# RWKV inverse on folded 64x64 blocks in two array quarters, with sample products and chunk products in another order

## The chip, the cores and the metric

One core of a Trainium2 chip runs the kernel. The metric is the device time of the execution in microseconds: the median of 3 runs is 2621.8 us (2618.93 to 2631.11).

## What is computed

One layer of a streaming encoder on 256 prompt tokens and 8 sequences of 16 sample tokens (384 columns in all), D_MODEL 2048: RMSNorm, one combined input projection, an RWKV-7 branch (16 heads of 64), a latent-attention branch, gates, output projection, and a ConvGLU of width 5632. The change touches the RWKV branch alone. Its recurrence, for every head with a 64x64 state S:

```python
def step(S, inp):
    r_t, w_t, k_t, v_t, kk_t, a_t = inp
    sa = jnp.einsum('bhvk,bhk->bhv', S, kk_t)
    S = (S * w_t[:, :, None, :] + v_t[..., None] * k_t[:, :, None, :]
         - sa[..., None] * (kk_t * a_t)[:, :, None, :])
    return S, jnp.einsum('bhvk,bhk->bhv', S, r_t)
```

## The kernel before

The kernel does not step through tokens. It takes the prompt in 4 chunks of 64 tokens and the 8 sample sequences as chunks of 16. Within a chunk the effect of the a-term is a unit triangular matrix of token by token, whose inverse is needed. It is built by doubling: a block-diagonal inverse of blocks of 2, then 4, 8, 16, 32, 64, in five levels.

**The slice loop.** 16 heads are taken two at a time, one head in each half of the 128 partitions. `pe_rwkv` (L374), `act_rwkv` (L573) and `dve_rwkv` (L693) are the body of a slice on PE, ScalarE (ACT) and VectorE (DVE). It runs 8 times: 7 in a hardware loop, once more behind it with other projections beside it. All in it is fp32, except the projections.

**The pieces.** Beside a slice PE computes the projection columns of later slices, so that it has work while the others answer. `pieces(n)` (L1168) issues n of a slice's 32 pieces; each is 2 k-tiles of `pe_block` (L828), with three passes of 384 columns each (w_hi with x_hi L836, w_hi with x_lo L837, w_lo with x_hi L838). Four pieces use up half a weight tile. Its split is done on ACT (`act_hi` L816, L821) and DVE (`dve_lo` L823, L826), at `cut(k)`: eight per slice and engine, in the order written out by hand. The split of a half waits for the half two before it to be used; SP loads the raw half when the split on DVE is done with the last one. ACT also takes finished projections out of PSUM at even cuts. Where a `pieces(n)` stands in `pe_rwkv` decides what PE does while a wait runs; their order is fixed by hand. Before, they stand as 2, 1, 1, then one in each of five levels, 2, one in each of four chunks, 1, 2, 2, 4 and 8.

**The inverse.** A unit is one head i (0, 1) and one token tile t of 128 (t 0 and 1 hold two prompt chunks each, t 2 the samples): 6 units, 128x128, block-diagonal with two 64x64 blocks. L394 makes the strictly lower products of beta and alpha (64 rows, 128 columns out and in), L401 those of kappa and alpha. DVE masks the first into t_y (L709, L710) and n_t (L707). t_y is the inverse so far, t_x its transpose; both are kept up. PE transposes t_y (L315) and ACT copies it into t_x (L582). A level then is: G = n_t' t_x (L418), one piece, DVE masks G into t_g (L718), the update of t_x (L429, subtracted at L723) and that of t_y (L433, subtracted at L726), directly behind which stands the next level's G. Levels 0 to 2 take all 6 units, 3 and 4 only the prompt's 4; the last level updates t_y alone. Every product is 128x128 on the whole array. Then L438 makes c_k and c_b, masked by DVE.

**The chunks.** For each chunk c: r (L456, L459), a piece, u from the inverse (L471), and for both heads the state gain (`gain`, L483 and L490, 64 rows and 64 partitions out) and the output (`yo`, L484, L486, L488, L493, 128 rows and 64 partitions out). Chunk 0 has the samples' parts too: L464, L465, L477, L498, L499 and eight 16-column products a head (L501). L508 makes the samples' state gains in chunks 1 and 2. DVE turns r (L738), u (L750) and the state (L755 to L764) around between them.

**The samples' first products.** L388 multiplies 8 states with 16 columns each, for head 0 and then head 1, each into its own half of the output partitions.

Of the kernel before, what the change touches and what calls it, by code (L numbers as in the profile page):

```python
# [21 lines left out]
P = 128  # L22
# [25 lines left out]
C2 = ["bones", "st64", "st64", "st16", "in64", "in64", "in16", "nl1", "lv2", "lv4", "lv8", "lv16", "lv32"]  # L48
C3 = ["rot"]
NC1 = len(C1) * P  # L50
NC2 = len(C2) * P + NT + 8
# [13 lines left out]
def constants():  # L65
# [30 lines left out]
    out = cat(C1) + cat(C2) + [reset, bm] + cat(C3) + [np.cos(ang), np.sin(ang), amask]  # L96
# [25 lines left out]
def build(nc, a, consts, outs):  # L122
# [28 lines left out]
    with ctx:  # L151
# [26 lines left out]
        cm = {n: c2[:, i * P:(i + 1) * P] for i, n in enumerate(C2)}  # L178
        reset = c2[:, len(C2) * P:len(C2) * P + NT]
        bmask = c2[:, len(C2) * P + NT:NC2]  # L180
# [20 lines left out]
        n_t, t_x, t_y, t_g, m_t, c_k, c_b = [  # L201
            region(n, [P, 6, P]) for n in ("n_t", "t_x", "t_y", "t_g", "m_t", "c_k", "c_b")]
# [10 lines left out]
        half = lambda t, h: t[:, 3 * h:3 * h + 3, :].rearrange("p u c -> p (u c)")  # L213
        yb, yc, sq_y, rn_y = half(t_g, 0), half(t_g, 1), half(t_x, 0), half(t_x, 1)
# [86 lines left out]
        BON = cm["bones"]  # L301
# [40 lines left out]
        units = lambda lv: [(i, t) for t in range(3 if lv < 3 else 2) for i in range(2)]  # L342
# [8 lines left out]
        each = lambda m, n: m.unsqueeze(1).unsqueeze(1).to_broadcast([P, 2, n, P])  # L351
        both = lambda m: m.unsqueeze(1).to_broadcast([P, 2, 3, P])
# [21 lines left out]

        def pe_rwkv(f, pieces, more=True):
# [30 lines left out]
            for i, t in units(0):  # L406
                last = transpose(head_tile(2, i, t), t_y[:, 3 * i + t, :])
            last.then_inc(E("t_x_ps"), 1)
            pieces(1)
            pe.wait_ge(E("nt_done"), f + 1)  # L410
            for lv in range(5):
                if lv == 0:
                    pe.wait_ge(E("t_x_done"), f + 1)
                else:
                    pe.wait_ge(E("t_done"), f * 9 + (2 * lv - 1))
                for i, t in units(lv):
                    u = 3 * i + t
                    last = mm_(head_tile(g_bank(lv), i, t), n_t[:, u, :], t_x[:, u, :], start=True, stop=True)  # L418
                last.then_inc(E("g_ps"), 1)
                pieces(1)  # L420
                pe.wait_ge(E("g_done"), f * 5 + (lv + 1))
                if lv == 0:
                    pe.wait_ge(E("mt_done"), f + 1)
                else:
# [6 lines left out]
                for i, t in units(lv):  # L431
                    u = 3 * i + t
                    last = mm_(head_tile(2, i, t), t_g[:, u, :], t_y[:, u, :], start=True, stop=True)  # L433
                last.then_inc(E("dt_ps"), 1)

            for b, src in ((4, kp_), (6, be)):
                for i, t in units(0):
# [3 lines left out]
            pe.wait_ge(E("t_done"), f * 9 + 9)  # L441
# [7 lines left out]
            for c in range(4):  # L449
# [20 lines left out]
                for i in range(2):  # L470
                    last = mm_(ps[r0:r0 + 64, 3, heads(i)], t_y[:, 3 * i + t, cs], rr[:, 0, heads(i)],  # L471
                               start=True, stop=True)
                last.then_inc(E("u_ps"), 1)
                if c == 0:
                    pe.wait_ge(E("rd_done"), f + 1)
                    for i in range(2):
                        last = mm_(ps[:, 7, heads(i)], t_y[:, 3 * i + 2, :], rr[:, 1, heads(i)], start=True, stop=True)  # L477
# [15 lines left out]
                mm_(yo[1], un[:, 0, heads(1)], c_b[:, 3 + t, cs], start=False, stop=True).then_inc(E("y_ps"), 1)  # L493
                if c == 0:
                    pe.wait_ge(E("ud_done"), f + 1)
                    for i in range(2):
# [3 lines left out]
                        for b in range(NB):  # L500
# [32 lines left out]
            pieces(8)  # L533
# [39 lines left out]
        def act_rwkv(f, cut, ch, more=True):  # L573
# [7 lines left out]
            act.wait_ge(E("t_x_ps"), f + 1)  # L581
            fn(t_x[:, :, :].rearrange("p (h t) c -> p h (t c)", h=2), ps[:, 2:4, 0:NT], ACT.Copy).then_inc(E("t_x_done"), 1)  # L582
# [4 lines left out]
            cut(2)  # L587
# [7 lines left out]
            cut(3)  # L595
# [1461 lines left out]
```

## Time and profile before

| what | value |
|---|---|
| median of 3 runs | 2621.8 us |
| profiled execution | 2617.77 us |
| its span, first to last instruction | 2616.1 us |
| PE busy | 2551.1 us, 98% |
| DVE busy | 1201.2 us, 46% |
| ACT busy | 848.4 us, 32% |
| GpSimd (POOL) busy | 108.4 us, 4% |
| mean granted TensorE clock | 0.995 |
| products of the inverse's levels L418, L433, L429 (records) | 416, 416, 352 |

In a window's row stand its start and end, its length, the busy time of PE, PEld, DVE, ACT and POOL with their instructions in brackets, the granted clock, the DMA share and GB/s.

Times in the rows are microseconds from the start of the span. PE is TensorE's matmul, PEld its weight load, which runs beside it. In the timeline a row is one instruction or a run of like ones: start, length from the first start to the last end, engine, line, what is written and read, the shape (array rows x columns used, then the moving operand), and the count. Matmuls overlap: the pitch from start to start is what one costs in a stream, and the length has its latency too.

### The profile page before, as it was taken

Reading aid. Unit: us, or ns where it says so; the run is one execution under the profiler, and the core shown is the slowest. Engines: PE = TensorE matmul, PEld = TensorE weight load, DVE = VectorE, ACT = ScalarE, POOL = GpSimd, SP = SyncE. Lnnn points to the kernel's source line nnn. Section 1 sums busy time; section 2 is a strip of 40 time slices with the busy share of each in tenths; the row PEclk is TensorE's granted clock in tenths of the full one; section 3 lists DMA queues with packets and bytes.
Section 4 is the critical chain, followed back from the end, with each engine's and each line's share of the span. In section 5 each row is a group of like instructions: output and inputs, shape, how many; then the busy total and the mean of one; then the engine's idle time right before and its main releaser. Section 6 shows DMA issues by size and latency. Waiting matters only on the chain.

```text
span 2616.1 us, 40662 instructions
## 1 busy us (share of the span) xinstructions
PE 2551.1 (98%) x15484; PEld 2353.6 (90%) x15484; DVE 1201.2 (46%) x1855; ACT 848.4 (32%) x1247; POOL 108.4 (4%) x182
## 2 busy tenths in 40 slices
PE   6999999999999999999999899999999999999997
PEld 6888888888888999999987799999878999999886
DVE  4566566665644333334433444444333444444233
ACT  4332233322223333334422433333222333333232
POOL 3000000000001010000000000000000000000010
PEclk9999999999999999999999999999999999999999
DMA  5321222212244343334453344444333444444443
GB/s 171 90 63 43 55 68 69 67 40 60 61 104 123 104 121 101 102 90 129 127 168 121 96 128 127 123 127 128 121 121 130 127 125 124 128 128 126 143 126 129
DMA packets 414494, 283.46 MB, mean 108 GB/s; under 512 B 31729, under 2 KB 392691, under 8 KB 413409
## 3 DMA queue, kind: packets, MB, share of 16 engines
q1 hardware_dynamic: 405600, 259.16, 33.7%
q0 software_dynamic: 8832, 23.43, 3.1%
q8 instruction: 46, 0.75, 0.1%
q14 instruction: 16, 0.12, 0.0%
HBM read 275.62 MB, written 6.92 MB: 108 GB/s over the span
## 4 chain that ended last, share of the span: by engine, by line
PE 95%; DVE 3%; ACT 1%; issue 1%; DMA 1%; POOL 0%; DVEq 0%; SPq 0%; POOLq 0%; ACTq 0%
PE banks L1392 19%; PE banks L836 17%; PE banks L838 17%; PE banks L837 17%; PE banks L315 2%; PE banks L418 2%; PE banks L429 2%; PE banks L433 2%; PE banks L847 2%; PE banks L848 2%; PE banks L849 2%; PE banks L484 1%; PE banks L483 1%; PE banks L1255 1%; PE banks L508 1%
## 5 line engine op out<-in xcount | busy, mean ns | idle before, releaser
L826 DVE TENSOR_TENSOR w_lo<-w_raw,w_hi 128x1024 fp32r<-128x1024 f32 x482 | 590.2, 1225 | 978.2 <-ACT w_hi L821 976.5
L836 PE MATMUL banks<-x_hi,w_hi 128*128 128x384 f32 x2640 | 910.0, 345 | 7.4 <-DVE w_lo L826 7.4
L838 PE MATMUL banks<-x_hi,w_lo 128*128 128x384 f32 x2640 | 883.4, 335 | 0.0
L837 PE MATMUL banks<-x_lo,w_hi 128*128 128x384 f32 x2640 | 882.9, 334 | 0.0
L821 ACT ACTIVATE w_hi<-w_raw 128x1024 fp32r<-128x1024 f32 x482 | 511.2, 1061 | 1041.2 <-PE banks L838 605.1
L836 PEld LDWEIGHTS banks<-x_hi,w_hi 128*128 128x128 f32 x2640 | 496.0, 188 | 22.6 <-DVE w_lo L826 9.3
L837 PEld LDWEIGHTS banks<-x_lo,w_hi 128*128 128x128 f32 x2640 | 496.3, 188 | 4.8
L838 PEld LDWEIGHTS banks<-x_hi,w_lo 128*128 128x128 f32 x2640 | 495.6, 188 | 0.0
L1392 PE MATMUL banks<-w_hi,act_hi 128*128 128x512 f32 x528 | 164.0, 392 | 4.7 <-DVE h_rows L1951 2.4
L1392 PE MATMUL banks<-w_hi,act_lo 128*128 128x512 f32 x528 | 163.9, 392 | 0.0
L1392 PE MATMUL banks<-w_lo,act_hi 128*128 128x512 f32 x528 | 163.7, 391 | 0.0
L1392 PEld LDWEIGHTS banks<-w_hi,act_hi 128*128 128x128 f32 x528 | 98.8, 188 | 27.3 <-issue 3.8
L1392 PEld LDWEIGHTS banks<-w_hi,act_lo 128*128 128x128 f32 x528 | 99.2, 188 | 21.7
L1392 PEld LDWEIGHTS banks<-w_lo,act_hi 128*128 128x128 f32 x528 | 99.2, 188 | 21.5
L1392 PE MATMUL banks<-w_hi,mix_hi 128*128 128x512 f32 x192 | 60.4, 396 | 4.5 <-DVE mix_lo L1938 3.0
L1480 ACT ACTIVATE proj_pad<-banks 128x256 f32<-128x256 f32 x24 | 9.2, 384 | 158.2 <-PE banks L838 158.2
L1392 PE MATMUL banks<-w_hi,mix_lo 128*128 128x512 f32 x192 | 60.1, 394 | 0.0
L1392 PE MATMUL banks<-w_lo,mix_hi 128*128 128x512 f32 x192 | 59.9, 393 | 0.0
L418 PE MATMUL banks<-t_x,n_t 128*128 128x128 f32 x416 | 54.4, 278 | 0.0
L433 PE MATMUL banks<-t_y,t_g 128*128 128x128 f32 x416 | 53.5, 276 | 0.0
L418 PEld LDWEIGHTS banks<-t_x,n_t 128*128 128x128 f32 x416 | 49.6, 192 | 2.5 <-issue 1.9
L429 PEld LDWEIGHTS banks<-t_g,t_y 128*128 128x128 f32 x352 | 41.7, 191 | 11.1 <-issue 7.6
(390 smaller groups left out, 2606.5 us busy)
## 6 DMA issues: line engine op xcount, KB each, us to landing
w_raw<-in_w_ffn_in SPq DMA_DIRECT2D x176, 512.0 KB, 4.0
w_raw<-in_w_in SPq DMA_DIRECT2D x144, 512.0 KB, 3.8
w_raw<-in_w_ffn_down SPq DMA_DIRECT2D x88, 512.0 KB, 3.6
w_raw<-in_w_out SPq DMA_DIRECT2D x32, 512.0 KB, 3.6
w_raw<-in_w_o_a SPq DMA_DIRECT2D x16, 512.0 KB, 3.9
w_raw<-in_w_o_b SPq DMA_DIRECT2D x16, 512.0 KB, 3.9
w_raw<-in_w_in SPq DMA_DIRECT2D x20, 256.0 KB, 3.7
w_ukv_head<-in_w_ukv POOLq DMA_DIRECT2D x8, 512.0 KB, 4.2
```

Of the source, the lines that this page charges most:

```text
L315: return nc.tensor.transpose(out, in_, ident[0:n, 0:n])
L418: last = mm_(head_tile(g_bank(lv), i, t), n_t[:, u, :], t_x[:, u, :], start=True, stop=True)
L429: last = mm_(head_tile(10 - g_bank(lv), i, t), t_y[:, u, :], t_g[:, u, :], start=True, stop=True)
L433: last = mm_(head_tile(2, i, t), t_g[:, u, :], t_y[:, u, :], start=True, stop=True)
L821: nc.scalar.activation(hi[:, s], raw[:, s], ACT.Copy).then_inc(hi_done, 1)
L826: nc.vector.tensor_tensor(lo[:, s], raw[:, s], hi[:, s].bitcast(F32), ALU.subtract).then_inc(lo_done, 1)
L836: nc.tensor.matmul(out, hi[:, s, k, :], xh[:, kt, :], start=kt == 0, stop=False)
L837: nc.tensor.matmul(out, hi[:, s, k, :], xl[:, kt, :], start=False, stop=False)
L838: last = nc.tensor.matmul(out, lo[:, s, k, :], xh[:, kt, :], start=False, stop=kt == 15)
L847: nc.tensor.matmul(out, hi[:, s, k, :], xh_[:, k, :], start=k == 0, stop=False)
L848: nc.tensor.matmul(out, hi[:, s, k, :], xl_[:, k, :], start=False, stop=False)
L1392: last = mm_(ps[:, 2 + 2 * t + cb, :], l_, w_[:, 512 * cb:512 * cb + 512], start=kt == 0 and n == 0, stop=kt == kts - 1 and n == 2)
```

## The change

- The 64x64 diagonal blocks of a unit are handled one by one: `blocks(lv)` gives (i, t, j), and block j lies in partitions 64j to 64j+63 and in 64 columns. t_x, t_y, t_g and n_t shrink to 64 columns a unit ("folded"), and so do the masks and DVE's work on them. Block j uses the rows and the output partitions of half j, two different quarters of the array.
- The second form is not updated by a product of its own: t_x alone is updated in levels 0 to 3, then transposed by a product with the identity (`turned`), and ACT copies it to t_y. The last level updates t_y, and DVE writes the result into t_full (t_f), 128 columns wide with zeros outside the blocks; ACT puts the samples' part there at level 3. The chunks read t_f.
- Pieces stand as 2, 1, 1, then G, 1, X, 1 in levels 0 to 3 and G, 1, Y in level 4, then 2, four of 1, 1, 2, 2, 4 and 4. Waits behind a piece are now issued ahead of its last pass (`at_last`).
- L388 and L501 alternate heads. In a chunk the outputs come first, all of 128x64, then the state gains, all of 64x64; y_ps is released ahead of state_ps and DVE no longer waits for it.
- The cuts are moved to fit, on ACT and DVE.

```diff
+        units = [(i, t) for t in range(3) for i in range(2)]
+        blocks = lambda lv: [(i, t, j) for t in range(3 if lv < 3 else 2) for i in range(2) for j in range(2)]
+        small = lambda b, i, t, j: ps[64 * j:64 * j + 64, b + i, 64 * t:64 * t + 64]
...
+        def turned(out, in_, j):
+            return nc.tensor.matmul(out, in_, ident[heads(j), heads(j)], start=True, stop=True)
...
-            for i in range(2):
-                for b in range(NB):
+            for b in range(NB):
+                for i in range(2):
                     mm_(ps[heads(i), 5, 16 * b:16 * b + 16], s0t[:, b, :],
                         al[:, i, 256 + 16 * b:272 + 16 * b], start=True, stop=True)
...
-            for i, t in units(0):
-                last = mm_(head_tile(6, i, t), be[heads(i), tile_tok(t)], al[heads(i), i, tile_tok(t)],
-                           start=True, stop=True)
+            for i, t, j in blocks(0):
+                own = slice(128 * t + 64 * j, 128 * t + 64 * j + 64)
+                last = mm_(small(6, i, t, j), be[heads(i), own], al[heads(i), i, own], start=True, stop=True)
...
-            pieces(1)
-            pe.wait_ge(E("t_first_done"), f + 1)
-            for i, t in units(0):
-                last = transpose(head_tile(2, i, t), t_y[:, 3 * i + t, :])
-            last.then_inc(E("t_x_ps"), 1)
-            pieces(1)
-            pe.wait_ge(E("nt_done"), f + 1)
+            pieces(1, lambda: pe.wait_ge(E("t_first_done"), f + 1))
+            for i, t, j in blocks(0):
+                last = turned(small(2, i, t, j), t_y[heads(j), 3 * i + t, :], j)
+            last.then_inc(E("form_ps"), 1)
...
+            pieces(1, matrix_ready)
             for lv in range(5):
...
+                if lv:
+                    for i, t, j in blocks(lv - 1):
+                        last = turned(small(2, i, t, j), t_x[heads(j), 3 * i + t, :], j)
+                    last.then_inc(E("form_ps"), 1)
+                for i, t, j in blocks(lv):
+                    u, h = 3 * i + t, heads(j)
+                    last = mm_(small(g_bank(lv), i, t, j), n_t[h, u, :], t_x[h, u, :], start=True, stop=True)
+                last.then_inc(E("g_ps"), 1)
+                pieces(1, level_ready)
+                if lv < 4:
+                    for i, t, j in blocks(lv):
+                        u, h = 3 * i + t, heads(j)
+                        last = mm_(small(10 - g_bank(lv), i, t, j), t_y[h, u, :], t_g[h, u, :], start=True, stop=True)
                 else:
-                    pe.wait_ge(E("t_done"), f * 9 + 2 * lv)
-                if lv < 4:
-                    for i, t in units(lv):
-                        u = 3 * i + t
-                        last = mm_(head_tile(10 - g_bank(lv), i, t), t_y[:, u, :], t_g[:, u, :], start=True, stop=True)
-                    last.then_inc(E("dt_ps"), 1)
-                for i, t in units(lv):
-                    u = 3 * i + t
-                    last = mm_(head_tile(2, i, t), t_g[:, u, :], t_y[:, u, :], start=True, stop=True)
+                    for i, t, j in blocks(lv):
+                        u, h = 3 * i + t, heads(j)
+                        last = mm_(small(2, i, t, j), t_g[h, u, :], t_y[h, u, :], start=True, stop=True)
                 last.then_inc(E("dt_ps"), 1)
+                if lv < 4:
+                    pieces(1, lambda: pe.wait_ge(E("t_done"), f * 5 + (lv + 1)))
...
                 for i in range(2):
-                    mm_(gain[i], tok[r0:r0 + 64, 0, t, heads(i)], v[r0:r0 + 64, t, heads(i)], start=True, stop=False)
                     mm_(yo[i], v[:, t, heads(i)], c_k[:, 3 * i + t, cs], start=True, stop=False)
-                    if c:
+                if c:
+                    for i in range(2):
                         mm_(yo[i], st[:, 1, :], rh[:, i, cols], start=False, stop=False)
                 pe.wait_ge(E("u_done"), f * 4 + (c + 1))
-                mm_(yo[0], un[:, 0, heads(0)], c_b[:, t, cs], start=False, stop=True)
+                for i in range(2):
+                    last = mm_(yo[i], un[:, 0, heads(i)], c_b[:, 3 * i + t, cs], start=False, stop=True)
+                last.then_inc(E("y_ps"), 1)
+                for i in range(2):
+                    mm_(gain[i], tok[r0:r0 + 64, 0, t, heads(i)], v[r0:r0 + 64, t, heads(i)], start=True, stop=False)
                 for i in range(2):
                     last = mm_(gain[i], tok[r0:r0 + 64, 1, t, heads(i)], un[r0:r0 + 64, 0, heads(i)],
                                start=False, stop=True)
                 last.then_inc(E("state_ps"), 1)
-                mm_(yo[1], un[:, 0, heads(1)], c_b[:, 3 + t, cs], start=False, stop=True).then_inc(E("y_ps"), 1)
...
-                        for b in range(NB):
+                    for b in range(NB):
+                        for i in range(2):
...
-            pieces(8)
+            pieces(4)
...
+            for lv in range(1, 5):
+                n = 3 if lv < 3 else 2
+                act.wait_ge(E("form_ps"), f * 5 + (lv + 1))
+                if lv == 3:
+                    for j in range(2):
+                        fn(t_f[heads(j), 2:6:3, heads(j)], ps[heads(j), 2:4, 128:192], ACT.Copy)
+                fn(by_head(t_y, n), made_small(2, n), ACT.Copy).then_inc(E("form_done"), 1)
+                if lv == 2:
+                    cut(2)
+            cut(3)
...
-                if lv == 1:
-                    cut(1)
+                if lv in (1, 3):
+                    cut(1 + lv // 2)
+                dve.wait_ge(E("dt_ps"), f * 5 + (lv + 1))
                 if lv < 4:
...
+                else:
+                    for j in range(2):
+                        h = heads(j)
+                        last = tt(by_head(t_f, 2)[h, :, :, h], by_head(t_y, 2)[h], made_small(2, 2, h), S)
+                    last.then_inc(E("t_done"), 1)
...
                 if c < 3:
-
-                    dve.wait_ge(E("y_ps"), f * 4 + (c + 1))
```

## Rows read from the trace of the kernel before

**Rows 1.** The page, part 1: busy time of each engine, share, instructions
```profile
PE 2551.1 (98%) x15484; PEld 2353.6 (90%) x15484; DVE 1201.2 (46%) x1855; ACT 848.4 (32%) x1247; POOL 108.4 (4%) x182
```
**Rows 2.** The page, part 4: the chain that ended last, by engine
```profile
PE 95%; DVE 3%; ACT 1%; issue 1%; DMA 1%; POOL 0%; DVEq 0%; SPq 0%; POOLq 0%; ACTq 0%
```
**Rows 3.** Windows (length, five engines' busy us, clock, DMA share, GB/s): a turn; its inverse
```profile
352.60:435.50 82.90, 82.59 (x650) 72.59 (x649) 50.71 (x88) 24.68 (x42) 5.19 (x8) 1.00 0.22 60
359.19:387.41 28.22, 27.94 (x221) 25.68 (x220) 17.06 (x19) 5.12 (x7) 0.00 (x0) 1.00 0.13 37
```
**Rows 4.** Timeline of PE at the first products and a level of the inverse
```profile
358.93 0.34 PE L838 MATMUL banks<-x_hi,w_lo 128*128 128x384 f32 x1
359.19 0.94 PE L394 MATMUL banks<-alpha_pad,beta 64*128 64x128 f32 x12
...
360.73 0.45 PE L836 MATMUL banks<-x_hi,w_hi 128*128 128x384 f32 x1
361.02 0.34 PE L837 MATMUL banks<-x_lo,w_hi 128*128 128x384 f32 x1
...
366.35 0.34 PE L838 MATMUL banks<-x_hi,w_lo 128*128 128x384 f32 x1
366.68 1.60 PE L429 MATMUL banks<-t_g,t_y 128*128 128x128 f32 x12
368.12 1.50 PE L433 MATMUL banks<-t_y,t_g 128*128 128x128 f32 x12
369.46 1.50 PE L418 MATMUL banks<-t_x,n_t 128*128 128x128 f32 x12
```
**Rows 5.** Timeline of chunk 1 and the start of chunk 2
```profile
401.45 0.34 PE L838 MATMUL banks<-x_hi,w_lo 128*128 128x384 f32 x1
401.72 0.45 PE L471 MATMUL banks<-r_rhs,t_y 128*64 128x64 f32 x4
402.10 0.32 PE L483 MATMUL banks<-tok_major 64*64 64x64 f32 x2
402.20 0.29 DVE L750 TENSOR_SCALAR u_neg<-banks 64x128 f32<-64x128 f32 x1 [1.32 <-PE banks L471]
...
402.98 0.27 PE L484 MATMUL banks<-c_k,tok_major 128*64 128x64 f32 x1
403.00 0.27 PE L488 MATMUL banks<-c_b,u_neg 128*64 128x64 f32 x1
...
403.36 0.33 PE L490 MATMUL banks<-u_neg,tok_major 64*64 64x64 f32 x4
...
403.62 0.64 PE L508 MATMUL banks<-v_by_sequence,tok_major 128*64 128x512 f32 x1
...
404.93 0.28 PE L459 MATMUL banks<-state,alpha_pad 128*64 128x64 f32 x2
...
405.14 0.45 PE L836 MATMUL banks<-x_hi,w_hi 128*128 128x384 f32 x1
```
**Rows 6.** Timeline of PE at the sample products
```profile
354.50 1.83 PE L388 MATMUL banks<-alpha_pad,s_t 128*64 128x16 f32 x32
...
397.33 0.32 PE L498 MATMUL banks<-c_k,tok_major 128*64 128x128 f32 x1
...
398.98 1.05 PE L501 MATMUL banks<-rho_pad,s_t 128*64 128x16 f32 x16
```
**Rows 7.** Timeline of DVE: a product over 384 and a mask over 768 columns
```profile
357.59 0.56 DVE L704 TENSOR_TENSOR bonus<-banks,z 128x384 f32<-128x384 f32 x1 [5.04 <-ACT alpha_s L579]
...
365.67 0.96 DVE L718 TENSOR_TENSOR t_g<-banks,consts_rwkv 128x768 f32<-128x768 f32 x1 [1.80 <-PE banks L418]
```
**Rows 8.** Timeline of DVE: u of chunk 3
```profile
412.28 0.29 DVE L750 TENSOR_SCALAR u_neg<-banks 64x128 f32<-64x128 f32 x1
```
**Rows 9.** Timeline: the end of the next slice's front on DVE, PE's first use
```profile
429.15 0.18 DVE L650 COPY proj_last_rkv<-proj_pad 128x24 f32 x1
...
436.33 0.49 PE L315 MATMUL banks<-consts_all,kappa 128*128 128x128 f32 x3
```

More of the change, by code:

```diff
@@ L95, in constants @@
     amask = np.where(key // 64 <= q // 64, 0, -1e30)
-    out = cat(C1) + cat(C2) + [reset, bm] + cat(C3) + [np.cos(ang), np.sin(ang), amask]
+    own = 64 * (s // 64) + np.arange(64)[None]
+    folded = [np.take_along_axis(np.asarray(m[n], f), own, 1) for n in C2_FOLDED]
+    out = cat(C1) + cat(C2) + folded + [reset, bm] + cat(C3) + [np.cos(ang), np.sin(ang), amask]
     return np.ascontiguousarray(np.concatenate([np.asarray(a, f) for a in out], 1))
@@ L200, in build @@
         kp_ = region("kappa", [P, NT])
-        n_t, t_x, t_y, t_g, m_t, c_k, c_b = [
-            region(n, [P, 6, P]) for n in ("n_t", "t_x", "t_y", "t_g", "m_t", "c_k", "c_b")]
+        n_t, t_x, t_y, t_g = [region(n, [P, 6, 64]) for n in ("n_t", "t_x", "t_y", "t_g")]
+        t_f, m_t, c_k, c_b = [region(n, [P, 6, P]) for n in ("t_full", "m_t", "c_k", "c_b")]
         tok = region("tok_major", [P, 3, 3, P])
@@ L212, in build @@
         assert top[0] <= 229368, top[0]
-        half = lambda t, h: t[:, 3 * h:3 * h + 3, :].rearrange("p u c -> p (u c)")
-        yb, yc, sq_y, rn_y = half(t_g, 0), half(t_g, 1), half(t_x, 0), half(t_x, 1)
+        yb, yc, sq_y, rn_y = [t[:, :, :].rearrange("p u c -> p (u c)") for t in (t_g, t_y, n_t, t_x)]
         x_off = (229368 - 4 * 3 * D) // 32 * 32
@@ L350, in build @@
         made = lambda b, n: ps[:, b:b + 2, 0:n * P].rearrange("p h (t c) -> p h t c", t=n)
-        each = lambda m, n: m.unsqueeze(1).unsqueeze(1).to_broadcast([P, 2, n, P])
-        both = lambda m: m.unsqueeze(1).to_broadcast([P, 2, 3, P])
+        each = lambda m, n: m.unsqueeze(1).unsqueeze(1).to_broadcast([P, 2, n, 64])
+        both = lambda m: m.unsqueeze(1).to_broadcast([P, 2, 3, m.shape[2]])
         GROUP = (1, 0, 2)
@@ L470, in pe_rwkv @@
                 for i in range(2):
-                    last = mm_(ps[r0:r0 + 64, 3, heads(i)], t_y[:, 3 * i + t, cs], rr[:, 0, heads(i)],
+                    last = mm_(ps[r0:r0 + 64, 3, heads(i)], t_f[:, 3 * i + t, cs], rr[:, 0, heads(i)],
                                start=True, stop=True)
@@ L476, in pe_rwkv @@
                     for i in range(2):
-                        last = mm_(ps[:, 7, heads(i)], t_y[:, 3 * i + 2, :], rr[:, 1, heads(i)], start=True, stop=True)
+                        last = mm_(ps[:, 7, heads(i)], t_f[:, 3 * i + 2, :], rr[:, 1, heads(i)], start=True, stop=True)
                     last.then_inc(E("ud_ps"), 1)
@@ L826, in dve_lo, with pe_block @@
             nc.vector.tensor_tensor(lo[:, s], raw[:, s], hi[:, s].bitcast(F32), ALU.subtract).then_inc(lo_done, 1)
-        def pe_block(t, s, out, ks=range(8), beside_norm=False):
+        def pe_block(t, s, out, ks=range(8), beside_norm=False, at_last=None):
             if ks[0] == 0:
@@ L837, in pe_block @@
                 nc.tensor.matmul(out, hi[:, s, k, :], xl[:, kt, :], start=False, stop=False)
+                if at_last and k == ks[-1]:
+                    at_last()
                 last = nc.tensor.matmul(out, lo[:, s, k, :], xh[:, kt, :], start=False, stop=kt == 15)
@@ L1166, in _, with pieces @@
                 done = 0
-                def pieces(n):
+                def pieces(n, at_last=None):
                     nonlocal done
@@ L1180, in _, with last_pieces @@
             done = 0
-            def last_pieces(n):
+            def last_pieces(n, at_last=None):
                 nonlocal done
@@ L1502, in act_cut, with cut @@
             def act_cut(f):
-                def cut(k, part=None):
+                def cut(k):
                     q, s = divmod(k, 2)
                     t = f * 4 + (T_FT + 4 + q)
-                    if s == 0 and part != 1:
+                    if s == 0:
                         if q == 0:
@@ L1522, in _, with last_cut @@
                 act_rwkv(f, act_cut(f), ch)
-            def last_cut(k, part=None):
+            def last_cut(k):
                 q, s = divmod(k, 2)
                 t = T_MLA + q
-                if s == 0 and part != 1:
+                if s == 0:
                     if k == 0:
```

98 lines of the change are left out of this document (46 added, 52 removed).

## The prediction

> **What bounds the kernel now.** I read the engines' busy time first: TensorE (PE) is busy for 2551.1 us of the 2616.1 us span, VectorE (DVE) for 46% of it [rows 1], and the chain that ended last is 95% PE [rows 2]. So a microsecond counts only if it leaves PE's stream. Then the windows: one turn of the slice loop lasts 82.9 us (PE 82.59 us busy, DVE 50.71, clock 1.00), of which 28.22 us lie between the first product of the inverse (L394) and the first of c_k (L438) [rows 3]. The loop's body runs 8 times. Last the timeline, since all that changes is how tightly small products stand in PE's stream and what a change of their shape costs. An fp32 product is two passes there, each with its own weight load; a "pass" below is one such record.
>
> **Prices of a pass, from rows.** (a) Full array, 128 columns out and in: 12 passes of L433 start 1.34 us before the next group, 0.112 us each [rows 4]. (b) Products with 64 output partitions, one after another in one half: L501's 16 passes last 1.05 us, the last 0.21 of it, so about 0.056; L388's 32 passes with a change of half in the middle fit [rows 6]. I take 0.058. (c) Alternate halves run beside each other: L484 of one head and L488 of the other start 0.02 us apart, and the four passes of L490 (two heads) last 0.33 us together where one is 0.22, so the last starts only 0.11 after the first [rows 5]. A pair thus costs what one costs, 0.058. (d) A change of array shape. Into a narrow shape the first start comes 0.27 us after the last wide one instead of 0.17 (+0.10; between narrow shapes L471's fourth pass starts at 401.945 and L483 0.15 later instead of 0.06, +0.09), and the second pass 0.05 late (L483: x2 lasts 0.32, so 0.10 apart). Out of it, L836 starts 0.15 us after L459's second pass instead of 0.06 (+0.09) [rows 5], and the next wide pass comes 0.29 us after it instead of 0.18 (+0.11) [rows 4]. One visit to a narrow shape costs 0.34 us. (e) One piece of projection (6 wide passes) is 1.04 us.
>
> **The inverse.** Removed: in 28.22 us stand 7 pieces (7.3 us), so 20.9 us of small products and waits. Some of it is idle time: from L838 to L429 0.33 us instead of 0.18 [rows 4], since a mask over 768 columns takes DVE 0.96 us [rows 7]; there are five such levels, plus the waits before the first transposes.
> Added: 64x64 products, two per old one, one in each diagonal quarter. Passes come in pairs: 12 for L394's successor, 12 for the first second-form, then G, X, and (form, G, X) for four levels with 12, 12, 12, 8, 8 products (a form has its previous level's size). That is 160 pairs behind the first group: 160 x 0.058 = 9.3 us. They lie in 11 visits: form; G0; X0; form+G1; X1; form+G2; X2; form+G3; X3; form+G4; X4: 11 x 0.34 = 3.8 us. The first group with the unchanged kappa products was 1.65 us (359.19 to 360.73, and 0.11 behind it [rows 4]); its 12 pairs at 0.058 with one shape change more (the kappa products keep 128 columns) make it 1.8. Sum 14.9 against 20.9: **6.0 us saved a turn.**
> This supposes that pairs of **diagonal** quarters overlap like (c). No row shows just that: L490's pair shares rows, L394's shares columns (12 passes last 0.94 us, the last 0.27 of it: 0.06 each, where the full array has 0.112 [rows 4]). Both halves of it overlap, so I take full overlap; the other end, none, is the first rival.
> Four pieces more stand between the products (p5, p7, p9, p11), taken from the tail; their 4.2 us are moved, not added. They must hide the new hand-overs. After G the mask covers 384 columns, 0.56 us like L704 [rows 7]. From G's last start: 0.22 to its end (a narrow pass: L490's 0.33 less 0.11 [rows 5]), 0.04, 0.56, 0.05: ready at 0.87. The piece's sixth pass, which now waits for it (at_last), would start at 0.15+0.29+4x0.174 = 1.14, its load 0.17 earlier: 0.1 us to spare. X to t_x is the same sum. ScalarE's copy of the second form has a whole G and a piece. VectorE's weight split (1.22 us) stands behind g_done at levels 1 and 3: it ends about 2.1 us after G's last start, X about 2.3. So no wait; I take off 0.3 us a turn for the edges of nine such waits (0 to 1.5).
>
> **The chunks.** Chunk 1 shows six shape changes (128x64, 64x64 and back) between L471 and L508. From L471's last start (401.945) to L508's first pass are 1.68 us [rows 5]. After: c_k and state products of both heads in parallel, 4 slots (0.23); then c_b must wait for u. u_neg is ready at 402.20+0.29+0.05 = 402.54, 0.60 after L471, where the products would be ready at 0.29: a wait of 0.3 us that L483/L484 covered before. Then 2 slots, into 64x64 (0.15), second pass 0.11, 3 slots, out (0.15): 1.24 us. Saved 0.44 for chunks 1 and 2. In chunk 0 u has L477 as cover: no wait, 0.55 saved with its changes. In chunk 3 u_neg starts only at 412.28, behind DVE's own scan and state work [rows 8]; PE stands and wins 0.18 only. The state update hangs on the gains, which now come last, but L508 stands behind them as before (its first pass alone 0.64 us), for a DVE chain of some 0.8 us. Sum **1.6 us** (1.0 to 2.2). The dropped wait on y_ps is worth nothing: state_ps came last there for chunks 1 to 3, and chunk 0 has L498 to L501 as cover.
>
> **Sample products.** L388: 32 passes, first to last start 1.62 us; as 16 alternating pairs 0.93: **0.7**. L498 to L501: 397.33 to 399.82, 2.49 us [rows 6]; after, 4 passes of 0.109 per head side by side (the second head one behind, 0.55) and 16 pairs (0.93): **1.0**. Bounds 1.3 to 1.8 together.
>
> **At no cost.** The smaller constants, one more memset, the two small copies into t_full (ScalarE is 30% busy), the two-part last update (0.85 us on DVE for 0.69; PE has 1.5 us of c products and two pieces before it needs it). The weight splits are moved with the pieces: each still comes within the four pieces ahead of its own. SP's next load is released by a split, as before; it now brings its 8 blocks in 74 us instead of 83, at a DMA share of 0.22 [rows 3]. POOL's loads for the next slice start after copies late in the turn and are used a turn later.
>
> **Sum.** 6.0 - 0.3 + 1.6 + 1.7 = 9.0 us a turn, 72 us for 8. The profiled execution took 2617.8 us (span 2616.1), so 2545.5; the median of the runs stands 4.0 us above it, and I put the new one between: **2548 us**.
>
> **Rival 1: the quarters take turns.** Both quarters of a unit write the same bank, in different partitions, from different rows of the array. L394's two row halves write banks 6 and 7, and L490's pair into one bank shares its rows, so no row shows this case, and none refutes turns. If they take turns, 172 pairs (160 and the first 12) cost 0.058 more each: 10.0 us a turn, 80 us, so 2628 us, no change. The rows that exist lean to overlap: chance 0.08. The Trainium skill, TensorEngine Tiling (Array Packing), section Restrictions and Gotchas, says that different row tiles cannot access one PSUM bank at the same time; by that rule the folding would win nothing, and no trace here shows it.
>
> **Rival 2, slower: each hand-over between quarters drains like a change of shape** (0.09 us). Place: the 172 products of the blocks. Price 172 x (0.058+0.09) = 25 us a turn, 204 us: 2752. The gain (9.0 us) is used up from 0.05 us extra per product, and the time is outside the noise from 0.06. For: nothing but the shape changes; against: L394 alternates rows without any. Chance 0.03.
>
> **Rival 3: lost cover.** (a) DVE finishes its work for the next slice at 429.33, PE asks at 436.33 [rows 9]: 7.0 us of cover, of which four pieces (4.2) leave, and about 1 us goes since ScalarE takes a projection before the split that DVE then waits for. 1.9 us remain; were the chain 3 us longer than I read it, 1.1 us in each of 7 turns would be lost, 8 us: 2556. (b) The sixth pass of a piece waits after all: 0.3 us at nine places, 2.7 a turn, 22 us: 2570. Together chance 0.08; still faster.
>
> **How the numbers follow.** Forecast 0.81, rivals 0.08, 0.03, 0.08. The terms' ends: edges 0 to 1.5, chunks 1.0 to 2.2, samples 1.3 to 1.8, and the visit of 0.34 us, pieced together from four starts, 0.08 either way (11 times, 0.9). Together 5.9 to 10.9 us a turn, and 8 turns off 2620 (what 2548 and 72 come from) give 2573 to 2533; this holds rival 3 as well and leaves out rivals 1 and 2. A measurement of this kernel can tell about 0.5% (13 us) from no change, so: faster 0.89, same 0.08, slower 0.03.
>
> **What would show it.** Right: block products with pairs of starts some 0.01 us apart and 0.058 from pair to pair; 26.4 us (14.9, and 11 pieces at 1.04) from the first block product to c_k; a turn of about 74 us with PE still near 99%; DVE u_neg as the releaser of c_b. Wrong: starts 0.058 apart for every pass (rival 1), 0.15 between quarters (rival 2), idle PE at front_done or before a piece's last pass (rival 3).

## The result, and the profile after

| what | before | after |
|---|---|---|
| median, runs of one comparison | 2628.31 us (6) | 2607.33 us (6) |
| lowest to highest | 2618.93 to 2637.86 us | 2603.29 to 2612.60 us |
| ratio, 95% interval | | 0.9925 (0.9899 to 0.9951) |
| profiled execution, its span | 2617.77, 2616.1 us | 2603.29, 2601.6 us |
| mean granted clock of the profiled execution | 0.995 | 0.980 |

Faster by 0.75%, with an interval wholly below 1, but the forecast said 2.8%; 2607 us lies far above the range (2533 to 2573). The page of after, parts 1, 3 and 4, against [rows 1, 2]:

```profile
PE 2499.0 (96%) x16908; PEld 2288.2 (88%) x16908; DVE 1140.6 (44%) x1832; ACT 861.2 (33%) x1295; POOL 108.7 (4%) x182
...
q8 instruction: 103, 1.69, 0.3%
...
PE 93%; DVE 3%; issue 2%; ACT 1%; DMA 1%; POOL 0%; DVEq 0%; SPq 0%; POOLq 0%; ACTq 0%
```

PE is busy 52 us less, as hoped, but the span fell by 14.5 us only: PE now has more idle time, and "issue" has doubled in the chain. One line of part 3 is worth a look that I did not give it. In before, the queue that brings the engines' instructions has this row:

```profile
q8 instruction: 46, 0.75, 0.1%
```

46 packets have become 103. The windows of the first two turns of the slice loop (columns as in [rows 3]), and the stretch behind the head of the second:

```profile
107.00:180.80 73.80, 72.16 (x828) 60.96 (x827) 43.15 (x87) 26.29 (x48) 5.80 (x10) 1.00 0.26 71
180.80:262.40 81.60, 75.41 (x827) 63.63 (x827) 43.14 (x85) 26.28 (x48) 5.09 (x9) 0.96 0.23 63
...
180.80:186.50 5.70, 1.06 (x8) 0.85 (x8) 0.00 (x0) 0.00 (x0) 0.12 (x1) 1.00 0.57 142
186.50:190.00 3.50, 3.50 (x36) 2.81 (x36) 0.00 (x0) 1.13 (x1) 0.00 (x0) 0.50 0.02 5
190.00:194.00 4.00, 4.00 (x25) 3.57 (x27) 1.78 (x2) 1.64 (x3) 0.00 (x0) 0.59 0.00 0
```

**The first turn came out as forecast**, 73.8 us for 82.9 ("about 74"). The six others of the loop take 80.1 to 81.9 us, with as many products on PE (826 to 828). The timeline of PE at the head of the first turn and of the second:

```profile
107.04 0.49 PE L320 MATMUL banks<-consts_all,kappa 128*128 128x128 f32 x3
107.37 0.49 PE L320 MATMUL banks<-consts_all,beta 128*128 128x128 f32 x3
107.70 0.49 PE L320 MATMUL banks<-consts_all,z 128*128 128x128 f32 x3
108.12 1.11 PE L399 MATMUL banks<-alpha_pad,s_t 128*64 128x16 f32 x32
...
180.82 0.52 PE L320 MATMUL banks<-consts_all,kappa 128*128 128x128 f32 x3 [0.51 <-issue]
181.18 0.49 PE L320 MATMUL banks<-consts_all,beta 128*128 128x128 f32 x3
181.50 0.38 PE L320 MATMUL banks<-consts_all,z 128*128 128x128 f32 x2
186.50 0.48 PE L320 MATMUL banks<-consts_all,z 128*128 128x128 f32 x1 [4.62 <-issue]
186.91 1.90 PE L399 MATMUL banks<-alpha_pad,s_t 128*64 128x16 f32 x32
```

PE stands for 4.62 us between two transposes of one group. No wait lies between them; "issue" means that no semaphore held it. Then the granted clock is 0.50, the 1.2 GHz level, and L399 takes 1.90 us instead of 1.11. The second turn is 7.8 us longer than the first: 4.6 us of standing, and the other 3.2 us go with the slow clock. The 0.5 us ahead of its head lie in the window of the first turn, which would last 73.3 us without them. The DMA part of after for 178 to 262 us has the row below; the same stretch of before (187 to 270 us) has no row of that queue at all.

```profile
q8 instruction: 10, 0.16, 0.8%
```

A loop of seven turns jumps back six times, and 57 packets more are 9.5 a jump. The trace also has the time of each packet: one starts at 178.2 us, behind the jump, and the next only at 183.7 us; it is through at 185.2 us, and PE stands from 181.9 to 186.5 us. So the reading: PE's code is fetched anew behind each jump. The six turns behind the first last 44.3 us more than six like it, most of the 59 us that the forecast lacks.

The rest of the first turn, term by term. Inverse: the first block products (L406) and the kappa products, a second form, G of level 0, the form and G of level 1, and c_k:

```profile
112.09 0.58 PE L406 MATMUL banks<-alpha_pad,beta 64*64 64x64 f32 x24
112.60 0.94 PE L412 MATMUL banks<-alpha_pad,kappa 64*128 64x128 f32 x12
...
114.71 0.91 PE L384 MATMUL banks<-consts_all,t_y 64*64 64x64 f32 x24
115.56 0.45 PE L864 MATMUL banks<-x_hi,w_hi 128*128 128x384 f32 x1
...
116.81 0.92 PE L438 MATMUL banks<-t_x,n_t 64*64 64x64 f32 x24
117.65 0.45 PE L864 MATMUL banks<-x_hi,w_hi 128*128 128x384 f32 x1
...
120.99 0.91 PE L384 MATMUL banks<-consts_all,t_x 64*64 64x64 f32 x24
121.74 0.87 PE L438 MATMUL banks<-t_x,n_t 64*64 64x64 f32 x24
122.54 0.45 PE L864 MATMUL banks<-x_hi,w_hi 128*128 128x384 f32 x1
...
138.12 0.94 PE L455 MATMUL banks<-rho_pad,kappa 64*128 64x128 f32 x12
```

24 passes of G begin 0.84 us before the next piece (116.81 to 117.65); the forecast's prices give 12 pairs at 0.058, 0.05 for the late second pass and 0.09 for the way out, 0.84. The single records start in pairs, 6 to 7 ns apart, and the pairs 58 ns apart. L406 does better than the forecast: its 24 passes take 0.51 us and not 12 x 0.058 and a change. They start in fours, 6 to 7 ns apart, and the fours 58 ns apart. It alternates heads, which are its array rows, and blocks, which are its output partitions, so all four quarters run beside each other. From the first block product (112.09) to c_k are 26.03 us, forecast 26.4. No piece's sixth pass waits. In chunks 1 and 3:

```profile
151.57 0.34 PE L506 MATMUL banks<-c_b,u_neg 128*64 128x64 f32 x4 [0.15 <-DVE u_neg L781]
151.84 0.33 PE L509 MATMUL banks<-tok_major 64*64 64x64 f32 x4
152.00 0.28 PE L511 MATMUL banks<-u_neg,tok_major 64*64 64x64 f32 x4
152.22 1.08 PE L529 MATMUL banks<-v_by_sequence,tok_major 128*64 128x512 f32 x4
...
160.74 0.34 PE L506 MATMUL banks<-c_b,u_neg 128*64 128x64 f32 x4 [0.78 <-DVE u_neg L781]
```

The releaser of c_b (L506) is u_neg, as said, and in chunk 3 it is late.

### The profile page after: what moved, and what is told of

Read it like the earlier page. It is cut to its first block, busy times and chain, and to the rows that moved or that the text cites. A ratio compares the mean times of both kernels' runs of the same rounds, so it can differ in the third digit from the quotient of the medians.

```text
span 2601.6 us, 43441 instructions
## 1 busy us (share of the span) xinstructions
PE 2499.0 (96%) x16908; PEld 2288.2 (88%) x16908; DVE 1140.6 (44%) x1832; ACT 861.2 (33%) x1295; POOL 108.7 (4%) x182
## 4 chain that ended last, share of the span: by engine, by line
PE 93%; DVE 3%; issue 2%; ACT 1%; DMA 1%; POOL 0%; DVEq 0%; SPq 0%; POOLq 0%; ACTq 0%
PE banks L1424 19%; PE banks L864 18%; PE banks L865 17%; PE banks L868 17%; PE banks L320 2%; PE banks L877 2%; PE banks L878 2%; PE banks L879 2%; PE banks L384 1%; PE banks L438 1%; PE banks L444 1%; PE banks L1290 1%; PE banks L1287 1%; PE banks L1385 1%; PE banks L399 1%
## 5 line engine op out<-in xcount | busy, mean ns | idle before, releaser
L864 PE MATMUL banks<-x_hi,w_hi 128*128 128x384 f32 x2640 | 922.7, 350 | 8.2 <-DVE w_lo L854 8.2
L747 DVE TENSOR_TENSOR t_g<-banks,consts_rwkv 128x384 f32<-128x384 f32 (+1 forms) x40 | 20.2, 504 | 87.5 <-PE banks L438 87.5
L1729 ACT ACTIVATE act_hi<-act 128x384 f32 (+1 forms) x44 | 23.1, 525 | 87.0 <-DVE act L2002 87.0
L1424 PEld LDWEIGHTS banks<-w_hi,mix_hi 128*128 128x128 f32 x192 | 36.3, 190 | 13.3 <-issue 3.4
L877 PE MATMUL banks<-rwkv_out_hi,w_hi 128*128 128x384 f32 x128 | 47.9, 374 | 0.0
L878 PE MATMUL banks<-rwkv_out_lo,w_hi 128*128 128x384 f32 x128 | 45.8, 358 | 0.0
```

Of the source, the lines that this page charges most:

```text
L864: nc.tensor.matmul(out, hi[:, s, k, :], xh[:, kt, :], start=kt == 0, stop=False)
L877: nc.tensor.matmul(out, hi[:, s, k, :], xh_[:, k, :], start=k == 0, stop=False)
L878: nc.tensor.matmul(out, hi[:, s, k, :], xl_[:, k, :], start=False, stop=False)
L1424: last = mm_(ps[:, 2 + 2 * t + cb, :], l_, w_[:, 512 * cb:512 * cb + 512], start=kt == 0 and n == 0, stop=kt == kts - 1 and n == 2)
```

## The experiments

**1, 2 and 3: where PE's loop stands in its code.** All instructions that compute stay; only the loop head of PE's program is put at a chosen place within its instruction block (256 instructions; filler stands ahead of it), or the loop is written out seven times. Each packet of the instruction queue has 16 KB.

```diff
-            with pe.Fori(0, FT - 1) as f:
+            pe_only = bass.OrderedEngineSet([pe.engine])
+            with nc.Fori(0, FT - 1, engines=pe_only, head_slot={pe.engine: 0}) as f:
```

> The changed kernel, with the first instruction of PE's slice loop placed at slot 0 of a 256-instruction block; the loop itself is the same. Theory F (fetch): the loop body (some 1690 instructions on PE, 1340 before) now touches one block more than PE keeps together with the next one fetched ahead, so every turn after the first fetches its head again; at slot 0 the body touches 7 blocks and not 8, and the stalls at the head (0.5 and 4.6 us, and some 3 us of half clock behind them) are gone: all turns last 73.8 us like the first, time about 2603 - 7 x 7.8 = 2549 us. Theory D (data): PE waits at the head for the other engines' front of the slice; the place of the code changes nothing, 2603 us, turns of 81 us.

```diff
-            with pe.Fori(0, FT - 1) as f:
+            for f in range(FT - 1):
```

> The changed kernel with PE's seven loop turns written out, the other engines' loops unchanged. Theory F: straight code is fetched ahead, no stall at a slice's head; about 2549 us, if fetching ahead keeps up (108 KB in 74 us); instruction bytes rise to all of the code once. Theory D: 2603 us. A third possibility, that straight code is itself too fast for the fetch, would show gaps all over the slices.

The third has 128 in the place of 0.

> As the kernel with the loop head at slot 0, but at slot 128. The body (some 1690 instructions) then ends in the eighth block. Theory F: stalls at every turn's head as in the changed kernel, at another place behind the head (some 128 instructions in, after the sample products, and not 16), turns of about 81 us, about 2603 us. Theory D: no difference between slots 0 and 128, and the gap stays where it is.

Head at 0: 2560.56 us, ratio 0.9737 (0.9718 to 0.9756), every turn 73.07 to 73.11 us. Written out: 2557.01 us, 0.9716 (0.9695 to 0.9737), turns of 73.07 to 73.09 us. With the head at 0, its window of the second turn, and its timeline there:

```profile
180.70:253.80 73.10, 71.96 (x828) 61.06 (x827) 43.09 (x87) 26.31 (x48) 5.21 (x9) 1.00 0.25 68
```

```profile
180.67 0.49 PE L320 MATMUL banks<-consts_all,kappa 128*128 128x128 f32 x3
181.00 0.49 PE L320 MATMUL banks<-consts_all,beta 128*128 128x128 f32 x3
181.33 0.49 PE L320 MATMUL banks<-consts_all,z 128*128 128x128 f32 x3
181.75 1.11 PE L399 MATMUL banks<-alpha_pad,s_t 128*64 128x16 f32 x32
```

The standing and the slow clock are gone together, at the same work: the head is as in the first turn. Packets of the instruction queue, 49, nine fewer than after for each of six jumps, and none between 168 and 620 us. Written out there are 88, and none holds PE up: code that runs straight on is fetched in time. So it isn't the volume of code but the jump back. Both come out 8 to 12 us above the 2549 us expected; the paragraph on the sum says where that lies.

Head at 128, one run of 2561.64 us: 104 packets, so the code is fetched anew as in after, but the turns are 73.5 to 74.8 us, not the 81 expected. The head of its third turn:

```profile
255.89 0.52 PE L320 MATMUL banks<-consts_all,kappa 128*128 128x128 f32 x3 [1.06 <-issue]
```

Refetching is necessary for the loss, not sufficient. What fits both: the jump leads into a block that must be fetched (0.4 to 1.1 us of standing, in after as here), and the packet of the block behind it starts 4.7 to 5.7 us later. In after PE has 16 instructions of transposes before it stands again (3.8 to 4.9 us in the six turns); with the head at 128 it has half a block of work meanwhile.

One thing stays open: why the second block takes so long. In after the DMA engines are full just then, with a weight load and POOL's loads (299 and 364 GB/s from 181 to 183 us), and the packet starts right behind them. In the padded kernel of experiment 5, where such a load ends ahead of the first of the two packets, the second starts 3.1 us behind it. No run moves these loads by itself, so how much of the 4.6 us is theirs isn't shown.

**4: a hint for the jump.** The loop's code ahead of it is as in after, but a hint at the top of each turn (BRANCH_PREFETCH_HINT in the trace, seven times) names the jump ahead of time.

```diff
+            with nc.Fori(0, FT - 1, engines=pe_only, hint_back_edge=True) as f:
```

> The changed kernel with a hint at the top of PE's loop that names the branch back, so that its target can be fetched early. Theory F: the first block of the head is there in time; the stall of 0.5 us goes, and the one of 4.6 us at the next block goes only if the fetch runs on from the hinted block; 2549 if both go, about 2600 if only the first. Theory D: 2603 us.

2559.26 us, 0.9725 (0.9704 to 0.9746), turns 73.07 to 73.11, 49 packets: as good as the placed head. No packet starts between 155 and 615 us, so the hint doesn't bring the head back early, as I expected; with it the loop's code is never lost. Whether it does so by itself or by where the loop then stands, the trace doesn't show.

**5 and 6: the kernel before, with its loop made as long, and written out.**

```diff
+                        for _ in range(22):
+                            pe.wait_ge(E("zeroed"), 1)
```

(ahead of each `pe_block` in the loop's pieces: waits that are met already, two to an instruction, 352 instructions more a turn.)

> The kernel before, with 22 waits on a semaphore that is long there ahead of each piece in PE's slice loop (two go into one instruction, 352 more in the body): no product, transfer or order is changed, and the body gets as long as the changed kernel's (about 1690 instructions). Theory F (fetch): turns after the first get a stall at the head as in the changed kernel, 82.9 plus 5 to 8 us, some 2629 + 50 us. Theory D (the changed order makes the data late): the extra waits are dispatched behind work in the queue and cost little; turns stay near 82.9 us, or grow evenly, the first too, by what the waits cost themselves.

> Control: the kernel before, with PE's loop turns written out. Its body (about 1340 instructions) never stalled, so theory F expects 82.9 us a turn as before and the same time within 0.3%, so that what the straight and the placed versions win over the changed kernel comes from stalls that the change made. If straight code were faster in itself, this one would win too.

Padded: 2707.56 us, 1.0294 (1.0262 to 1.0325), 102 packets for 46, 1690 records of PE a turn. Written out: 2631.18 us, 1.0011 (0.9993 to 1.0030), turns of 82.6 us. The padded one's first two turns, and its second head:

```profile
104.90:194.80 89.90, 83.84 (x650) 72.67 (x648) 50.87 (x90) 24.68 (x42) 5.87 (x10) 1.00 0.25 67
194.80:289.50 94.70, 87.96 (x649) 76.04 (x650) 50.82 (x88) 24.67 (x42) 5.16 (x8) 0.95 0.20 54
```

```profile
194.79 0.88 PE L315 MATMUL banks<-consts_all,kappa 128*128 128x128 f32 x3 [4.18 <-issue]
...
197.45 0.47 PE L315 MATMUL banks<-consts_all,z 128*128 128x128 f32 x1 [0.73 <-issue]
```

The same standing appears in a kernel that has none of the change, once its loop is long enough. A window from head to head holds the standing ahead of the next head: 4.18 of the first turn's 89.90 us. Without it that turn takes 85.7, so the waits themselves cost 2.8 us a turn, 8 ns an instruction, where the expectation had little. The five turns with a jump at both ends last 94.7 to 96.0 us, 9.0 to 10.3 more than 85.7; the last, with a jump only ahead of it, 90.8. The standing is divided otherwise than in after, 4.18 us at the head and 0.73 at the next block, and here too the packet at the head (192.1 us) starts right behind a weight load. The two kernels thus differ in nothing of kind here; the body of before was short enough to stay, PE's records per turn being 1337 with the sequencer's, those of after 1687. In before no packet starts between 184 and 695 us.

**7: do the quarters need to alternate?** (On the version with the head at 0, as 10 to 12 too.)

```diff
-        blocks = lambda lv: [(i, t, j) for t in range(3 if lv < 3 else 2) for i in range(2) for j in range(2)]
+        blocks = lambda lv: [(i, t, j) for j in range(2) for t in range(3 if lv < 3 else 2) for i in range(2)]
```

> The changed kernel with the loop head at slot 0, and the block products in the order of quarters: all blocks of the upper quarter, then all of the lower, in each group. The same products and waits. If the two diagonal quarters run beside each other only when they alternate (my step c), each of the 172 pairs costs 0.058 us more: turns of 73.1 + about 9 us (a few products at the border still overlap), 83 us. If alternation gave nothing (the bank shared by both quarters), the turn stays 73.1.

One run, 2609.56 us, turns 79.21 to 79.23: 6.13 us a turn more, where I expected about 9 (the paragraph on rival 1 has the reason). G of level 0:

```profile
117.75 1.43 PE L438 MATMUL banks<-t_x,n_t 64*64 64x64 f32 x24
119.11 0.44 PE L864 MATMUL banks<-x_hi,w_hi 128*128 128x384 f32 x1
```

1.36 us for the same 24 passes instead of 0.84. Single records start 58 ns apart in it, except that three passes of the second half start beside the last ones of the first (0.14 + 21 x 0.058 = 1.36). The quarters overlap only where their passes stand within a few places of each other in the stream, and there they do, in one bank: rivals 1 and 2 fall.

**8 and 9: the edge, head at 96 and at 111.**

> The changed kernel with the loop head at slot 96 of a block. Theory F with blocks of 256 instructions: 96 + about 1690 ends within the seventh block (1792), so the loop is fetched once, as at slot 0: about 49 instruction packets and turns of 73.1 us. If it is the length alone and not the blocks touched, it behaves like slot 128: 104 packets and turns of 74 us.

> The changed kernel with the loop head at slot 111, 15 slots behind the placement that was fetched once. 111 + about 1690 is over 1792, the end of the seventh block, by a few instructions. Theory F with blocks of 256: the eighth block is touched and the loop is fetched again in every turn (about 100 instruction packets, against 50 at slot 96), though the stall may be short as at slot 128, since the first block holds 145 instructions of work. If blocks play no part, nothing differs from slot 96.

At 96 (2552.27 us, one run): 50 packets, turns 73.07 to 73.12. At 111 (2561.68 us, one run): 59 packets, not about 100, and one turn of seven with a standing of 1.41 us:

```profile
547.20 0.52 PE L320 MATMUL banks<-consts_all,kappa 128*128 128x128 f32 x3 [1.41 <-issue]
```

Between 96 and 128 the loop thus begins to lose its code, in one turn of seven at 111; why in that one isn't shown. Each of the two single times is worth no more than 1%; the turns are what counts.

**10 and 11: the terms of the chunks and of the samples undone.** The chunks' order and the wait on y_ps are as before; or L399 and L522 take one head after the other.

```diff
+                    mm_(gain[i], tok[r0:r0 + 64, 0, t, heads(i)], v[r0:r0 + 64, t, heads(i)], start=True, stop=False)
                     mm_(yo[i], v[:, t, heads(i)], c_k[:, 3 * i + t, cs], start=True, stop=False)
...
+                    dve.wait_ge(E("y_ps"), f * 4 + (c + 1))
```

> The changed kernel with the loop head at slot 0, and the chunk products back in the old order (gain and output alternating, y_ps last, VectorE's wait on it restored). My sum says 1.6 us a turn for the new order (0.55, 0.44, 0.44, 0.18 for the chunks): turns of 74.7 us against 73.1. If the shape changes cost nothing, 73.1.

```diff
-            for b in range(NB):
-                for i in range(2):
+            for i in range(2):
+                for b in range(NB):
...
```

(L522 in the same way.)

> The changed kernel with the loop head at slot 0, and the two groups of sample products back in the old order, head by head. My sum says 0.7 + 1.0 us a turn: turns of 74.8 us against 73.1.

Turns of 74.73 to 74.75 us (2570.54 us, one run) and of 74.95 to 74.99 us (2570.44 us, one run): the chunks' order is worth 1.66 us a turn, the samples' alternation 1.89.

**12: u first.** In chunk 3 DVE makes u_neg ahead of its scan and the samples' state update.

```diff
+                dve.wait_ge(E("u_ps"), f * 4 + (c + 1))
+                nc.vector.tensor_scalar(un[r, 0, :], ps[r, 3, 0:P], -1.0, None, M).then_inc(E("u_done"), 1)
-                elif c == 3:
+                if c == 3:
...
-                dve.wait_ge(E("u_ps"), f * 4 + (c + 1))
-                nc.vector.tensor_scalar(un[r, 0, :], ps[r, 3, 0:P], -1.0, None, M).then_inc(E("u_done"), 1)
```

> A version for speed: the changed kernel with the loop head at slot 0, and in chunk 3 VectorE makes u before its scan difference and the samples' state update and not behind them. The trace shows PE standing 0.78 us there in every slice. If that work is not needed at once by others, the gap goes to about 0.3 us (as in chunks 1 and 2): 73.1 - 0.5 us a turn, 4 us in all, about 2556; if the state update or the exponentials on ScalarE become late behind it, the time stays.

```profile
233.03 0.34 PE L506 MATMUL banks<-c_b,u_neg 128*64 128x64 f32 x4 [0.15 <-DVE u_neg L775]
```

The wait of chunk 3 fell from 0.78 to 0.15 us, but turns are 72.75 to 72.80 us, only 0.3 less than 73.08. Its time is 2556.37 us, 0.9710 (0.9684 to 0.9735), the lowest median of several runs, level with the loop written out (2557.01 us). Against head 0 its median is 4 us lower, but each has its own comparison and the intervals overlap; what is shown is the 0.3 us a turn.

Not tried: the value of issuing a wait ahead of a piece's last pass instead of behind the piece.

## Why the prediction was wrong in size and right in its terms

**The step that failed is "At no cost".** It lists constants, copies, splits, SP's and POOL's loads, and never PE's own instructions. The forecast counted each new product's 58 ns and not that its turn grows from 650 to 828 passes in a loop that is run from a store of limited size. Experiments 1 to 5 show the price: after's seven turns last 560.8 us together, with the head placed 511.6, so 49 us for six jumps. With the head placed the time is 2560.56 us, inside the forecast range. The ratios say the same, 0.9925 against 0.9737 (1.9 points of 2629 us, 49 us).

The trace of before could not show this stall, but it had its conditions: the row of the instruction queue, and no fetching inside the loop. The Trainium skill, Runtime: NRT & Kernel Launch, section Instruction fetch mechanics, has the rule: a taken branch whose target has left the engine's window of code forces a fetch before execution goes on. I did not weigh it. It would have given one more rival, "the loop outgrows its code store". After agrees with the rule, with nine packets a jump. The same section speaks of 2048 instructions for TensorE in blocks of 256, and of a window of two pages. By two pages the loop of before (1337 records) would have been fetched anew too, and it was not: 46 packets in all, none in the turn looked at. The larger figure, eight blocks, is nearer to these runs: by the count of records the body of after touches seven blocks from slot 0 or 96 and stays, and from 128 it reaches into an eighth and is lost; from 111 it does so by six instructions and was lost once. By that figure alone eight should stay too. That the block fetched ahead needs the eighth place is my inference, and no run tests it by itself.

**The inverse: right.** Forecast 6.0 - 0.3 us a turn. With the head placed a turn lost 82.90 - 73.08 = 9.82 us; less 1.66 and 1.89 (experiments 10 and 11) this leaves 6.3. The traces have it directly too: 28.22 us of before and four more pieces at 1.04 us against 26.03 us are 6.35. The price of a pair (0.058 us) and of a shape change held within 0.02 us in G of level 0, though the overlap of diagonal quarters stood in no row: that step was argued, and it held. The 0.3 us for edges was not needed, no piece's last pass waited, and L406 gave 0.2 us that the forecast didn't see, since it counted pairs where four quarters run.

**The chunks: right**, 1.6 forecast, 1.66 found (one run). That PE stands at u_neg in chunk 3 was seen; that two moved instructions of DVE give back 0.3 us was not taken up.

**The samples: right**, 1.7 forecast, 1.89 found (one run), just above the bounds (1.3 to 1.8), with 32 passes in 1.04 us in L399 and in 0.92 us in L522.

**Rival 1** fell. The page TensorEngine Tiling (Array Packing) of the Trainium skill, section Restrictions and Gotchas, rules out one bank for different row tiles at a time; here two quarters with different rows write different partitions of one bank 6 to 7 ns apart, and standing one behind the other they cost 6.1 us a turn more. Its price for a full serial order, 10.0 us, was above those 6.1 because the kernel in that order still overlaps at each change of half. The 15 groups of 160 pairs behind L406 and the four places where a G follows a form at once make 19 changes of three passes, 57 of the 160 passes that the alternation saves, and (160 - 57) x 0.058 = 6.0. L406 adds 0.17: in that order its passes still run in pairs, by its rows, 0.67 us for 0.51. Together 6.1, as measured.

**Rival 2** fell with it. **Rival 3**: (b) did not come; (a) neither, no turn waits for DVE at L320.

**The sum.** With the code's fetch taken out, 72 us forecast for eight turns. (2617.8 less 72 is 2545.8 and not 2545.5, which changes nothing.) The spans of head 0 and before, from the starts of like instructions: head 0 enters the loop 2.8 us later, wins 68.7 us in seven turns, stands 74.1 us ahead at the first product behind the eighth, 71.4 at its next transposes, and only 59.3 at the last layer's first wait (1286.2 against 1345.5 us); there it stays (59.4 at the end). Of the 2.8 us, after (2.3 us late) has 0.8 in a longer wait for the first split weights (2.68 us for 1.87); the rest I didn't follow. The 12.1 us fall in a stretch that the change doesn't touch. Windows of 50 us of before, then of head 0:

```profile
950.00:1000.00 50.00, 50.00 (x308) 47.72 (x306) 17.19 (x36) 17.33 (x33) 5.93 (x8) 1.00 0.46 127
1000.00:1050.00 50.00, 50.00 (x310) 47.65 (x309) 17.07 (x32) 14.20 (x25) 5.35 (x9) 1.00 0.38 106
```

```profile
900.00:950.00 50.00, 50.00 (x297) 47.71 (x296) 16.75 (x36) 16.51 (x31) 1.77 (x3) 0.97 0.40 110
950.00:1000.00 50.00, 50.00 (x280) 47.64 (x281) 16.97 (x32) 12.66 (x23) 5.37 (x9) 0.90 0.34 96
1000.00:1050.00 50.00, 50.00 (x287) 47.75 (x285) 14.51 (x30) 14.76 (x27) 3.58 (x6) 0.93 0.35 99
1050.00:1100.00 50.00, 50.00 (x305) 48.05 (x304) 16.51 (x20) 15.26 (x21) 0.00 (x0) 0.97 0.26 75
```

The missing clock is 50 x (0.03 + 0.10 + 0.07 + 0.03) = 11.5 us. Whether the change has a part in it stays open. Every kept trace of a changed version has such a dip between 900 and 1150 us, after too (0.97, 0.93, 0.90, 0.97), and so has the padded kernel (0.91, 0.93, 0.97 from 1100 to 1250 us); before has none there and before written out 0.97 twice. But before's own runs in these comparisons have a mean clock from 0.995 (2617 us) to 0.986 (2640 us), head 0's from 0.986 to 0.988, so before loses clock in some executions as well. The one profiled execution on which my sum stood (0.995) was at the favourable end, so 2620 was a low base; against before's median of 2629 us, head 0 saves 68.5 us where 72 were forecast.

## What to carry to other kernels

When a change trades few wide instructions for many small ones inside a hardware loop, count the engine's instructions per turn as well as their time, and look at the row of the instruction queue before and after: packets that grow with the number of turns mean that the loop no longer stays loaded. Then place the loop's head, hint the jump, or write the loop out; each of the three gave back 47 to 50 us here, for a line or two. And compare the first turn with the later ones: a cost that the first turn lacks doesn't lie in its work. When windows run from head to head, look at where the standing falls: that ahead of a head counts in the turn before, and read into the first turn it looks like work.

## What was not expected of the hardware

- Whether PE's loop of 1687 records was fetched anew went by its place: head at 0 or 96, 49 and 50 packets, never; 111, 59, once; 128, 104, and as first built, 103, at each jump. The loss per jump at the same number of packets was 8.2 us (49 by six) as built and 1.3 us at 128; what fits is how much code lies between the head and the next block.
- The standing of 4.6 us cost some 3.2 us more through the clock: 0.50 from 186.5 to 190 us and 0.59 to 194 us. With the head at 128 PE stood 1.06 us and the clock stayed at 1.00.
- 352 instructions of waits that were already met cost 2.8 us a turn, 8 ns each, on a PE that otherwise never stood.
- Four 64x64 quarters ran beside each other in L406: four fp32 passes start within 20 ns, and the next four 58 ns behind the first.
- The granted clock fell to 0.90 over 50 us in a stretch where PE was busy all of it, in after and head 0 and not in before, at like work. What decides it stays open.
